# Block substitution moved from VectorE to GpSimd, RWKV side work four places earlier, and the scan beside the seventh attention head one window later

## The reference, cut to what matters

```
sa    = state @ at
state = state * wt + sa bt^T + vt kt^T          # per head 64 x 64, for each of 1024 tokens
y     = state @ rt
```

## Time and profile before

| | us |
|---|---|
| runs, device time | 1707.43, 1712.31, 1717.62 (median 1712.31) |
| the profiled execution, device time | 1711.84 |
| its span | 1709.9 |
| TensorE, weight loads, VectorE, ScalarE, GpSimd busy | 1637.6, 1270.0, 1119.9, 874.8, 769.2 |

### The profile page before, as it was taken

How to read it: one execution, slowest core, us unless ns; L and a number is a source line. 1 busy time by engine, 2 the same in 40 slices (tenths; PEclk the granted TensorE clock), 3 DMA queues, 4 the chain that set the end, 5 groups by cost and what they waited for, 6 DMA issues and landing times.

```text
span 1709.9 us, 30411 instructions
## 1 busy us (share of the span) xinstructions
PE 1637.6 (96%) x11876; PEld 1270.0 (74%) x11876; DVE 1119.9 (65%) x1732; ACT 874.8 (51%) x1695; POOL 769.2 (45%) x555
## 2 busy tenths in 40 slices
PE   8999999988888889899999999999999999999997
PEld 6676777745577677688977667788888888888886
DVE  7744343435576775633787769887758856784788
ACT  5323233345425455511463467776667666656763
POOL 4210212011212012322492266877768695867771
PEclk9999999988999999999999999999999999999999
DMA  6100010001122222422302002020211203020202
GB/s 243 37 26 22 25 47 1 22 6 31 33 37 46 50 47 106 160 87 74 112 28 72 1 7 93 25 75 25 75 41 59 73 27 99 26 74 26 74 1 99
DMA packets 82842, 94.47 MB, mean 55 GB/s; under 512 B 53776, under 2 KB 56336, under 8 KB 82704
## 3 DMA queue, kind: packets, MB, share of 16 engines
q1 hardware_dynamic: 82704, 92.57, 17.3%
HBM read 82.57 MB, written 9.98 MB: 54 GB/s over the span
## 4 chain that ended last, share of the span: by engine, by line
PE 75%; DVE 13%; issue 3%; ACT 3%; DMA 3%; POOL 2%; SPq 1%; DVEq 0%; ACTq 0%; POOLq 0%
PE PS L1779 39%; PE PS L1063 8%; PE PS L978 5%; PE PS L1164 3%; PE PS L1203 2%; PE PS L1182 2%; PE PS L1735 2%; PE PS L1713 1%; PE PS L1566 1%; PE PS L1237 1%; DVE H L2993 1%; POOL sa L926 1%; DVE sa L2919 1%; DVE sc_s L2654 1%; DVE sc_s L2657 1%
## 5 line engine op out<-in xcount | busy, mean ns | idle before, releaser
L1779 PE MATMUL PS<-memr,wsp 128*128 128x512 f32 x1488 | 357.5, 391 | 1.1 <-DVE memr L2975 1.1
L1779 PEld LDWEIGHTS PS<-memr,wsp 128*128 128x128 f32 x1488 | 278.7, 188 | 63.2 <-DVE memr L2975 3.2
L941 POOL TENSOR_TENSOR wsp<-sa,wsp 128x512 fp32r<-128x512 f32 x120 | 164.4, 1373 | 167.9 <-ACT wsp L2227 167.7
L1779 PE MATMUL PS<-memr,wraw_r 128*128 128x512 f32 x744 | 180.1, 390 | 0.5 <-DVE memr L2975 0.5
L1779 PEld LDWEIGHTS PS<-memr,wraw_r 128*128 128x128 f32 x744 | 139.4, 188 | 31.1 <-DVE memr L2975 1.2
L1779 PE MATMUL PS<-tmp_r,wsp 128*128 128x512 f32 x564 | 147.2, 395 | 3.7 <-DVE tmp_r L2975 3.4
L1063 PE MATMUL PS<-xn,wsp 128*128 128x512 f32 x576 | 146.3, 400 | 2.5 <-DVE proj L2450 1.6
L2975 DVE TENSOR_TENSOR memr<-PS,memr 128x512 fp32r<-128x512 f32 x185 | 126.0, 681 | 34.2 <-ACT PS L2265 34.2
L832 POOL CAST wsp<-wraw 128x1024 fp32r<-128x1024 f32 x24 | 28.0, 1166 | 238.3 <-PE PS L1063 112.6
L2993 DVE TENSOR_TENSOR H<-PS,H 128x512 f32<-128x512 f32 x160 | 108.0, 686 | 39.7 <-PE PS L1779 24.3
L1914 ACT ACTIVATE H<-PS,mst 128x128 f32<-128x128 f32 (+3 forms) x64 | 47.5, 742 | 165.8 <-DVE mst L2534 165.8
(11 more groups left out here) (394 smaller groups left out, 3420.0 us busy)
## 6 DMA issues: line engine op xcount, KB each, us to landing
sa<-in_weights_dram SPq DMA_DIRECT2D x40, 512.0 KB, 4.3
wraw<-in_weights_dram SPq DMA_DIRECT2D x24, 512.0 KB, 3.8
sa<-in_weights_dram SPq DMA_DIRECT2D x48, 256.0 KB, 2.7
H<-in_x_dram SPq DMA_DIRECT2D x16, 512.0 KB, 7.7
sbx<-in_weights_dram SPq DMA_DIRECT2D x32, 256.0 KB, 2.8
H<-in_weights_dram SPq DMA_DIRECT2D x8, 512.0 KB, 6.9
out_dram<-sbx SPq DMA_DIRECT2D x16, 256.0 KB, 2.1
a_dram<-H SPq DMA_DIRECT2D x16, 128.0 KB, 2.5
```

The costliest lines, as they stand in the source:

```text
L941: nc.gpsimd.tensor_tensor(w[:, 1, :], w_source(g), w[:, 0, :].bitcast(F32), ALU.subtract).then_inc(mw_rest, 1)
L1779: last = nc.tensor.matmul(PS[:, bank_of(g), :], w[:, a, win(k)], x[:, b, :], start=(k == 0 and (a, b) == (0, 0)), stop=(k == ROWS - 1 and ...
```

## The change: what it does

1. The substitution, the clearing of X and the transposed copy are taken out of VectorE's `prep` and put into GpSimd's: clearing at slot 24, all 30 products and sums and the copy at slot 25, each waiting for the one before. By GpSimd's order they stand behind slot 22's products and ahead of the diagonals of group three. SyncE waits for GpSimd's copy.
2. `place_of` is replaced by `reached` and `slots_at`: in pairs two and three, each place does the slot four numbers on. In pair one the lead grows from 0 to 4 (one more at places 13, 22, 31 and 40, which do two slots each). Pair four keeps its own. The same holds for `post`, which goes by the slot.
3. On VectorE alone, beside the seventh head: behind window 3 only k's scaling; behind window 4 the scan and its input; behind window 5 slot 4 and 5's three instructions.

```diff
-SUBST = {26: (0, 1, 2, 3), 27: (4, 5, 6, 7), 28: (8, 9, 10, 11), 29: (12, 13), 30: (14,)}
+SUBSTITUTE = 25
+AHEAD = 4
...
+        def reached(p, s):
+            if p == PAIRS - 1:
+                return s
+            return s + (min(AHEAD, max(s - 4, 0) // 9) if p == 0 else AHEAD)
+        def slots_at(p, s):
+            last = reached(p, s)
+            first = last if s <= 4 else reached(p, s - 1) + 1
+            slots = [(p, x) for x in range(first, last + 1) if x < SLOTS]
+            if p == PAIRS - 2:
+                return slots + [(p + 1, s - SLOTS)] * (s >= SLOTS)
+            return slots + [(p + 1, x - SLOTS) for x in range(first, last + 1) if x >= SLOTS]
+        def vector_beside_heads(h, q):
+            if h == BESIDE and 3 <= q <= 5:
+                return ((3,), (4,), (5, 6, 7, 8, 9))[q - 3]
+            return beside_heads(h, q)
...                                     # SyncE
-                sp.wait_ge(P_DVE.sem, P_DVE.at(f"xt_{n}", -1))
+                sp.wait_ge(P_POOL.sem, P_POOL.at(f"xt_{n}", -1))
...                                     # GpSimd's prep; the same lines leave VectorE's
+                if s == 24:
+                    nc.gpsimd.memset(bX, 0.0) ...
+                    nc.gpsimd.memset(sc_s[:, 3456:3712:BLK + 1], 1.0) ...
+                if s == SUBSTITUTE:
+                    for j in range(BLK - 1):
+                        if j == 0:
+                            own(f"x1_{n}")
+                            pool.wait_ge(a_blocks_loaded, 16 * (n + 1))
+                        else:
+                            own(f"xa{j - 1}_{n}")
+                        shape = [P, BLK - 1 - j, j + 1]
+                        below, part = bX[:, j + 1:BLK, 0:j + 1], bT[:, j + 1:BLK, 0:j + 1]
+                        nc.gpsimd.tensor_tensor(part, bA[:, j + 1:BLK, j:j + 1].broadcast_to(shape),
+                                                bX[:, j:j + 1, 0:j + 1].broadcast_to(shape), ALU.mult) ...
+                        own(f"xm{j}_{n}")
+                        nc.gpsimd.tensor_tensor(below, below, part, ALU.add) ...
+                    own(f"xa{BLK - 2}_{n}")
+                    nc.gpsimd.tensor_copy(bXT, bX.rearrange("p i n -> p n i")) ...
...                                     # VectorE's prep
+                late = 0 if n else 1
-                if s == 3:
+                if s == 3 + late:       # t1p and the scan; slots 4 and 5 likewise
```

More of the change, by code:

```diff
@@ L527, in build @@
         P_DVE = Steps(sem("prep_dve"), each(
-            ["kk", "t1p", "L", "na", "am", "k2", "nkk", "at", "b", "bt", "kt", "al0", "al1", "al2", "al3", "rk", "x0", "x1"]
-            + [y for place in SUBST for j in SUBST[place] for y in (f"xm{j}", f"xa{j}")] + ["xt", "bv0", "bv1a", "bv1"]))
-        P_POOL = Steps(sem("prep_pool"), each(["rt", "kh", "bh"]))
+            ["kk", "t1p", "L", "na", "am", "k2", "nkk", "at", "b", "bt", "kt", "al0", "al1", "al2", "al3", "rk", "bv0", "bv1a", "bv1"]))
+        P_POOL = Steps(sem("prep_pool"), each(
+            ["rt", "kh", "bh", "x0", "x1"] + [y for j in range(BLK - 1) for y in (f"xm{j}", f"xa{j}")] + ["xt"]))
         O_PE = Steps(sem("post_pe"), each(["vs0", "vs1", "lg0", "lg1"]))
@@ L587, in places @@
             return range(11 * g + 7 + 2 * k, 11 * g + 9 + 2 * k)
-        def place_of(p, s):
-            return (p, s) if s < SLOTS else (p + 1, s - SLOTS)
+        def reached(p, s):
[9 more added lines that the diff above has]
+            return slots + [(p + 1, x - SLOTS) for x in range(first, last + 1) if x >= SLOTS]
         def beside_heads(h, q):
@@ L856, in prep, with own @@
                 wt = rW.rearrange("p (c t) -> p c t", c=NC)[:, :, CH - 1:CH].broadcast_to([P, NC, CH])
+                def own(name):
+                    pool.wait_ge(P_POOL.sem, P_POOL.at(name, -1))
                 if s == 17:
@@ L872, in prep @@
                                             ALU.mult).then_inc(P_POOL.sem, P_POOL.one(f"bh_{n}"))
+                if s == 24:
+                    if n >= 1:
+                        pool.wait_ge(x_blocks_stored, 32 * n)
+                    nc.gpsimd.memset(bX, 0.0).then_inc(P_POOL.sem, P_POOL.one(f"x0_{n}"))
+                    own(f"x0_{n}")
+                    nc.gpsimd.memset(sc_s[:, 3456:3712:BLK + 1], 1.0).then_inc(P_POOL.sem, P_POOL.one(f"x1_{n}"))
+                if s == SUBSTITUTE:
[8 more added lines that the diff above has]
+                        nc.gpsimd.tensor_tensor(part, bA[:, j + 1:BLK, j:j + 1].broadcast_to(shape),
+                                                bX[:, j:j + 1, 0:j + 1].broadcast_to(shape), ALU.mult).then_inc(
+                            P_POOL.sem, P_POOL.one(f"xm{j}_{n}"))
+                        own(f"xm{j}_{n}")
+                        nc.gpsimd.tensor_tensor(below, below, part, ALU.add).then_inc(P_POOL.sem, P_POOL.one(f"xa{j}_{n}"))
+                    own(f"xa{BLK - 2}_{n}")
+                    nc.gpsimd.tensor_copy(bXT, bX.rearrange("p i n -> p n i")).then_inc(P_POOL.sem, P_POOL.one(f"xt_{n}"))
             def value_split(u):
@@ L1529, in beside, with beside_slot @@
             def beside(p, s):
-                p, s = place_of(p, s)
-                if p == PAIRS:
-                    return
+                for pair, slot in slots_at(p, s):
+                    if pair < PAIRS:
+                        beside_slot(pair, slot)
+            def beside_slot(p, s):
                 if p >= 1:
@@ L2584, in prep @@
                     r(nc.vector.tensor_scalar(rKK, kk_, vec[:, V_KK + n:V_KK + n + 1], -1.0, ALU.mult, ALU.mult), "kk")
-                if s == 3:
+                late = 0 if n else 1
+                if s == 3 + late:
                     r_at(P_ACT, f"tw1_{n}")
                     r(nc.vector.tensor_scalar(rT1, rT1, 1.0, None, ALU.add), "t1p")
-                if s == 3:
+                if s == 3 + late:
                     own("t1p")
@@ L2592, in prep @@
                     r(nc.vector.tensor_tensor_scan(rWi, rStep, rT1, 0.0, ALU.mult, ALU.add), "L")
-                if s == 4:
+                if s == 4 + late:
                     r_at(P_ACT, f"ta1_{n}")
                     r(nc.vector.tensor_scalar(rA, rA, -0.5, -0.5, ALU.mult, ALU.add), "na")
-                if s == 4:
+                if s == 4 + late:
                     own("na")
                     r(nc.vector.tensor_scalar(rT1, rA, 1.0, vec[:, V_KA + n:V_KA + n + 1], ALU.add, ALU.mult), "am")
-                if s == 5:
+                if s == 5 + late:
                     own("am")
@@ L2638, in prep @@
                     r(nc.vector.scalar_tensor_tensor(r_, r_, vec[:, V_RK + n:V_RK + n + 1], rT1, ALU.mult, ALU.mult), "rk")
[L2639 to L2660, removed]
                 if s in (BONUS, BONUS + 1):
@@ L2784, in _ @@
                         filled(h, q)
-                        for s in beside_heads(h, q):
+                        for s in vector_beside_heads(h, q):
                             prep(0, s)
@@ L2789, in _ @@
                 filled(h, NW - 1)
-                for s in beside_heads(h, NW - 1):
+                for s in vector_beside_heads(h, NW - 1):
                     prep(0, s)
@@ L2795, in _ @@
                         evict_half(u, half)
-                for s in beside_heads(h, NW):
+                for s in vector_beside_heads(h, NW):
                     prep(0, s)
```

## The result

The changed kernel takes 1733.21 us (median of 6 runs, 1728.68 to 1735.70) against 1710.95 for the kernel before (6 runs): ratio 1.0132, interval 1.0112 to 1.0152. The prediction said 1711, with 1697 to 1724 as its range. It is wrong, and outside the range.

What follows compares the result with a forecast made beforehand. TensorE, not fed without a break in the attention and RWKV loops, was taken as the bound; -4.9 - 4.9 + 4.9 + 2.4 + 1.6 = -0.9 took 1711.84 to 1710.9, said as 1711 us, range 1697 to 1724.

Steps and rivals of the forecast that it cites:

- Scan and eighth head, -9.8: Attention loop: later scan in the seventh head gains 4.9 us, substitution out of the eighth head 4.9 us.
- GpSimd's price, S = 11.3: GpSimd's substitution: 11.3 us from A's blocks to the last sum, 8.6 for 30 instructions plus 2.7 of gaps.
- The matrix behind it, +8.4, +2.8, +2.8: RWKV loop: third group's transition matrix, waiting for GpSimd, comes later by 8.4 us in pair one, 2.8 in later pairs.
- Rival B: GpSimd's queue becomes the wait: substitution of 14.5 us or more costs over 9 us extra, 1722 at 15; chance 0.17.
- Third groups, -1.5, -1.3, -1.3: RWKV loop, third groups: shorter by 1.5 us in pair one, 1.3 in later pairs, state copy right behind the matrix.
- Fourth: -0.3: RWKV loop, fourth group: 0.3 us shorter, an estimate from durations of the trace's half products.
- First group: RWKV loop, first group: bound by TensorE, takes in A's 64 products moved forward, +1.2 us net.
- The ScalarE and GpSimd steps moved along have idle engines: RWKV loop, side steps moved earlier by the lead: their engines are idle; no time was given for them.
- the 0.8 that it takes off pair three: RWKV loop, pair three: same as pair two's +2.4 less 0.8 us, since pair four takes nothing early: +1.6.
- the groups that are not the second change by more than 2 us: RWKV loop: sign that the prediction is wrong as a whole, groups other than the second changing by over 2 us.
- rival D: RWKV loop: lead clears ends of groups, TensorE fills, 2 us per pair beyond the count, 1706; 0.42 together with forecast.

Runs made afterwards that it cites:

- first_on_pool: Kernel before with the later scan, and the substitution on GpSimd for the first pair only, no lead; 1699.25 us, ratio 0.9924.
- scan_only: Kernel before with the later scan (part 3 of the change) alone; 1709.08 us, ratio 0.9982.
- no_lead: Changed kernel with its lead set to 0, substitution on GpSimd and later scan kept; 1721.96 us, ratio 1.0065.
- lead_only: Kernel before with the lead of up to four places alone, substitution on VectorE, scan where it was; 1727.10 us, ratio 1.0082.
- short_scan: Changed kernel with the decay scan of pairs three and four over 128 of 1024 columns; 1728.41 us, ratio 1.0103.
- short_scale: Changed kernel with VectorE's four scaling steps of slots 14 to 16 over 128 of 1024 columns in pairs three and four; 1724.16 us, ratio 1.0083.

## Why the prediction was wrong, by its steps

*Scan and eighth head, -9.8.* Right in the sum. The maxima came where they were said: the first right behind its scores (374.88), TensorE's stand 2.52 instead of 6.42 us, window 7's maximum at 423.33. The first matrix is 8.8 us earlier, and first_on_pool has the whole kernel 13 us faster by its ratio (8.6 to 17.6). The split is less right: scan_only has 3.1 for the 4.9. The maximum over 512 keys (window 4, as the prediction counts) stands ahead of the changed work in both heads, and divides the gain; the seventh head before and after, then the eighth:

```profile
368.94 0.69 DVE L2534 TENSOR_REDUCE mst<-PS 128x1 f32<-128x512 f32 x1 [3.98 <-PE PS L1167]
370.59 0.69 DVE L2582 TENSOR_REDUCE mst<-PS 128x1 f32<-128x512 f32 x1 [3.98 <-PE PS L1211]
415.16 0.69 DVE L2534 TENSOR_REDUCE mst<-PS 128x1 f32<-128x512 f32 x1
412.56 0.69 DVE L2582 TENSOR_REDUCE mst<-PS 128x1 f32<-128x512 f32 x1
```

The changed kernel's execution was 1.7 us late there, so that between these two executions the loop gained 10.4: 4.3 up to the eighth head's window 4, and 6.2 from there to the first matrix. Over all the runs' traces the second stretch takes 50.0 to 51.2 us with the substitution on VectorE and 43.1 to 45.0 with it on GpSimd, 5 to 8 us where 4.9 was forecast; the first takes 43.4 and 46.2 with the old scan and, but for one of 45.2, 41.9 to 42.4 with the later one, 1 to 4 us where 4.9 was forecast. The sum came out partly because the two errors cancel. Below are the maxima of windows 5 and 7 after, and TensorE's stand.

```profile
374.88 0.82 DVE L2582 TENSOR_REDUCE mst<-PS 128x1 f32<-128x640 f32 x1 [0.30 <-PE PS L1211]
423.33 1.09 DVE L2582 TENSOR_REDUCE mst<-PS 128x1 f32<-128x896 f32 x1
```
```profile
378.10 1.20 PE L1284 MATMUL PS<-sa,con 128*128 128x512 f32 x2 [2.52 <-ACT sa L2010]
```

*GpSimd's price, S = 11.3.* Right: 10.7. The lines drawn from 256, 512 and 1024 elements hold down to 15: 0.20 us fixed gave 0.22 for the shortest product and 0.32 for a sum of 63 or 64 elements. By the rule of the Trainium skill (GPSIMD Engine Reference, Engine selection), twice VectorE's time, it would have been 12.5, an estimate, and the gaps of 2.7: this case doesn't bear it out for instructions so short, where the ratio is 1.3 (0.272 to 0.208 in the median, see the end).

*The matrix behind it, +8.4, +2.8, +2.8.* Nearly right: +6.7, +3.1, +2.2. Rival B's mechanism is there, at the size forecast. The measured 1733 is what rival B would give at an S of 18.7; S is 10.7, so it is not B that made the kernel slow.

*Third groups, -1.5, -1.3, -1.3.* Off: 0.0, +0.6, -1.1 after, while no_lead has -1.4, -2.2, -2.0. The state copy does come right behind the matrix; with the lead other steps may stand ahead of later ones, which no run took apart.

*"Fourth: -0.3. First group: it is TensorE's, and takes in the 64 products of A moved forward (two lots of 1.2 us): +1.2 net, the second group having the room. [...] The ScalarE and GpSimd steps moved along have idle engines"*. This step failed. Measured: fourth groups (2.1, 3.1) +3.5 and +3.9, first groups (2.2, 3.2) +5.8 and +5.6, 18.8 us where the forecast has -0.7 for the four (-2.0, +1.2, -0.3 and +0.4, if the 0.8 that it takes off pair three, at no named place, is taken off the first group). The two profiled executions are 24.0 us apart where the forecast has -0.9. Of this miss of 25 the four groups are 19.5 and the third groups 3.6; the matrix behind GpSimd takes 2.0 back, and the rest, about 4, lies mainly in pair one's first group (1.1), pair three's fourth (0.8), the attention loop (1.0) and behind the last matrix (1.6). The prediction counted what each group contains and not where in its engine's queue it stands. It even said what to look for ("the groups that are not the second change by more than 2 us"), and held rival D, that the lead would help by clearing the ends of groups; the ends are where long steps are free. no_lead and lead_only show that the lead is the cause, with either engine for the substitution; short_scan and short_scale that VectorE's long steps between chunk steps are most of it (6.0 us in the fourth groups and 10.0 in the first ones). In the fourth groups what waits behind them is the state copy, in the first groups the products of A, which read their result. How the rest divides between the clock and ScalarE's moved steps, which stand ahead of the copies that TensorE's chunk steps wait for (L2072, L2073), was not tried apart.

## What to carry to other kernels

A side step moved by hand is priced by what stands right behind it in its engine's queue, and by how soon an engine reaches the step that reads its result. Here a 2.3 us scan lay free ahead of an instruction that waits for another engine, and cost up to 4 us between the steps of a recurrence. If side work must come earlier, move it by a whole period of the loop it runs beside, so that each step keeps its neighbours: 4 of 11 places cost 11 to 14 us, 11 of 11 nothing that shows, and the group gained was the room that GpSimd's slow, dependent chain needed. Judge a transfer to an idle engine by what else that engine's queue must deliver next.

## What the runs showed of the hardware that was not expected

- A run of small dependent instructions on GpSimd costs 0.21 to 0.33 us each and 0.06 to 0.09 between, about 1.3 times VectorE's for the same products. The forecast from larger rows held within 6%. The 60 products after, by line (min/median/max ns):

```profile
L910 POOL TENSOR_TENSOR sc_s<-sc_s x60: 215/272/308, 418.8 to 645.3; 128x15 f32<-128x15 f32 x8, 128x28 f32<-128x28 f32 x8, 128x39 f32<-128x39 f32 x8, 128x48 f32<-128x48 f32 x8
```
- The granted clock fell behind short stands of TensorE: it stood 2.76 us up to 522.67, and the stretch from 524 shows 0.55; it stood 2.02 us up to 543.03, and the stretch from 546 shows 0.50, at full busy time. Pair three's same two groups show 0.50 as well, from 602 and from 622. With the scaling steps cut, the stretch from 542 keeps 1.00. Such a stand is paid for twice, in the wait and in the slower work behind it.
